# A mixture-of-experts kernel in which experts of 128 and of 64 slots alternate

## The reference, cut to what matters

```python
def _clamped_swiglu(hgu):
    x_glu = jnp.minimum(hgu[..., ::2], SWIGLU_LIMIT)
    x_lin = jnp.clip(hgu[..., 1::2], -SWIGLU_LIMIT, SWIGLU_LIMIT)
    return x_glu * jax.nn.sigmoid(SWIGLU_ALPHA * x_glu) * (x_lin + 1.0)

def _moe_sequence(h, ...):
    logits = h @ w_router + b_router
    top_val, top_idx = lax.top_k(logits, TOP_K)
    gates = jax.nn.softmax(top_val, axis=-1)
    ...                      # rows sorted by expert, group_sizes rows each
    hgu = lax.ragged_dot(xs, w_gate_up, group_sizes) + b_gate_up[e_sorted]   # 1024 -> 2048
    act = _clamped_swiglu(hgu)
    out = lax.ragged_dot(act, w_down, group_sizes) + b_down[e_sorted]        # 1024 -> 1024
    out = out * gates...
    return jax.ops.segment_sum(out, tok, num_segments=L)
# after it: h = _layernorm(2**0.25 * h + moe, ln2_g, ln2_b)
```

## Time and profile before

| | |
|---|---|
| three runs | 1982.99, 1983.78, 1988.11 us (median 1983.78) |
| profiled execution | 1988.11 us |
| its span, first to last instruction | 1986.4 us |
| TensorE clock granted, mean | 0.983 of full speed |
| PE, DVE, ACT, POOL busy | 97%, 86%, 69%, 24% of the span |
| DMA | 533.04 MB, mean 268 GB/s |

### The profile page before, as it was taken

One profiled execution on the slowest core, in us unless ns is written; L12 is line 12 of the kernel. 1 busy time (PEld: TensorE's weight loads), 2 busy tenths in 40 slices (PEclk: granted clock), 3 DMA queues, 4 the chain that ended last, 5 costly groups with the idle time before them and its releaser, 6 DMA issues.

```text
span 1986.4 us, 29687 instructions
## 1 busy us (share of the span) xinstructions
PE 1934.8 (97%) x8812; PEld 1543.5 (78%) x8812; DVE 1704.4 (86%) x1768; ACT 1372.6 (69%) x1742; POOL 468.4 (24%) x339
## 2 busy tenths in 40 slices
PE   6999999998989999999999999999999999999998
PEld 3657767787768887888888888888888888888886
DVE  6899977358855478999999999999999999999998
ACT  4456855224345526888888888888888888888885
POOL 6671000000000108323222232222322222222231
PEclk7999999999989988999999999999999999999999
DMA  8222225332010257999999999999999999999995
GB/s 318 79 107 84 85 100 181 124 100 81 22 43 23 64 170 267 376 388 376 374 380 369 388 372 375 385 371 387 373 378 382 362 387 370 376 384 363 384 373 213
DMA packets 152207, 533.04 MB, mean 268 GB/s; under 512 B 14479, under 2 KB 19759, under 8 KB 149408
## 3 DMA queue, kind: packets, MB, share of 16 engines
q1 hardware_dynamic: 136112, 492.45, 65.6%
q0 software_dynamic: 16048, 39.99, 7.8%
HBM read 517.75 MB, written 24.26 MB: 273 GB/s over the span
## 4 chain that ended last, share of the span: by engine, by line
PE 89%; DVE 7%; DMA 1%; issue 1%; ACT 1%; SPq 0%; DVEq 0%; ACTq 0%
PE ps L980 55%; PE ps L1127 4%; PE ps L1175 4%; PE ps L918 3%; PE ps L1118 3%; PE ps L1156 2%; PE ps L1132 2%; PE ps L1351 2%; PE ps L1223 2%; PE ps L886 2%; PE ps L1017 2%; PE ps L857 1%; DMA arena<-in_w_down 1%; PE ps L1105 1%; PE ps L871 1%
## 5 line engine op out<-in xcount | busy, mean ns | idle before, releaser
L980 PE MATMUL ps<-split,xTs 128*128 128x512 f32 x3264 | 771.1, 392 | 0.7 <-ACT split L1799 0.5
L980 PEld LDWEIGHTS ps<-split,xTs 128*128 128x128 f32 x3264 | 610.8, 188 | 131.2 <-DVE split L2551 1.5
L2551 DVE TENSOR_TENSOR split<-arena,split 128x2048 fp32r<-128x2048 f32 x204 | 464.0, 2287 | 49.7 <-ACT split L1799 49.6
L1799 ACT ACTIVATE split<-arena 128x1024 fp32r<-128x1024 f32 x408 | 409.8, 1054 | 106.0 <-PE ps L980 104.6
L2551 DVE TENSOR_TENSOR split<-ring,split 128x2048 fp32r<-128x2048 f32 x204 | 465.7, 2314 | 0.4 <-ACT split L1799 0.3
L1799 ACT ACTIVATE split<-ring 128x1024 fp32r<-128x1024 f32 x408 | 410.9, 1055 | 66.7 <-PE ps L980 53.7
L980 PE MATMUL ps<-split,aTs 128*128 128x512 f32 x1632 | 385.9, 392 | 0.2 <-DVE split L2551 0.2
L980 PEld LDWEIGHTS ps<-split,aTs 128*128 128x128 f32 x1632 | 303.7, 188 | 63.4 <-DVE split L2551 0.9
L728 POOL DMA_INDIRECT arena<-h_rows,slots x33 | 92.8, 2811 | 340.0 <-PE ps L918 244.8
L776 POOL DMA_INDIRECT y_rows<-arena,slots x33 | 94.0, 2848 | 176.3 <-issue 104.9
L1961 DVE TENSOR_TENSOR split<-ring,split 128x2048 fp32r<-128x2048 f32 (+1 forms) x32 | 72.7, 2273 | 63.4 <-ACT split L1462 63.4
(11 more groups left out here) (437 smaller groups left out, 2539.0 us busy)
## 6 DMA issues: line engine op xcount, KB each, us to landing
ring<-in_w_gate_up SPq DMA_DIRECT2D x170, 1024.0 KB, 8.8
arena<-in_w_gate_up SPq DMA_DIRECT2D x102, 1024.0 KB, 7.3
arena<-in_w_down SPq DMA_DIRECT2D x102, 1024.0 KB, 10.3
ring<-in_w_down SPq DMA_DIRECT2D x34, 1024.0 KB, 10.8
ring<-in_w_in SPq DMA_DIRECT2D x23, 1024.0 KB, 5.0
ring<-in_w_out SPq DMA_DIRECT2D x8, 1024.0 KB, 5.4
ring<-in_mod_w SPq DMA_DIRECT2D x10, 512.0 KB, 9.1
ring<-in_mod_w SPq DMA_DIRECT2D x4, 1024.0 KB, 5.0
```

Of the source, the lines that this page charges most:

```text
L980: m = mm(ps[:, banks + q, :], lhs[:, x_, k, :], w[:, q * 512:(q + 1) * 512], start=start, stop=stop)
L1799: A(split[:, 0, c % SPLITS, :], chunk(c), ACT.Copy).then_inc(sig("hi_ready"), 1)
L2551: V.tensor_tensor(split[:, 1, s_, :].rearrange("p a b -> p (a b)"), chunk_pair(p), split[:, 0, s_, :].rearrange("p a b -> p (a b)"), ALU.s ...
```

## The change

1. The sixteen experts with the most rows (and expert 0 always) are *big*, 128 slots; the others are *small*, 64 slots. They alternate: item 0 big, then big and small in turn, then the last small one and, one by one, what is over (64 slots each) in a loop of its own. The code for an item is so laid down several times, the loop over 14 pairs of a big and a small item in the middle.
2. A small item has its 64 high columns and 64 low columns side by side in one stationary operand. One matmul then gives x_hi*w_hi and x_lo*w_hi in the upper and lower 64 rows of PSUM, a pair is 8 matmuls and not 12. Before the activation the halves are added: ACT copies PSUM to `comb` (`rows_out`), and 8 matmuls against two identities side by side (`turn_sum`) add and turn it at once. The activation of a half is then 128x256, already turned. The down product's two halves are not added but scattered one after the other, the second when the first has landed.
3. In a small item two of the down pairs (8 and 9, `WHOLE`) are not split: PE multiplies the chunks as plain fp32, 4 matmuls each.
4. Unused slots point out of bounds and are left out by the scatter. A small item gathers 64 rows.
5. The four down tiles are loaded as `(p k)`: each partition takes two neighbouring rows, a piece of 8 KB. The activation is turned to match.
6. The list of items by size comes from DVE (`key`, `max`, a scan) and one matmul, and DVE reads the order straight from PSUM. What is over is listed by POOL (`late_list`), once, in the middle of its loop.
7. `y_dram` begins as plain `h1` (4 DMAs, earlier). The gates are divided by `ALPHA` and the epsilon by its square. `gates@b_down` is added at the end, in the PSUM banks of the last sum.

```diff
+WHOLE = (8, 9)
@@ expert_tile
-                sp.dma_start(x..., src.rearrange("o (k p) n -> p (o k) n", p=P)).then_inc(tile_ready[j % SLOTS], 16)
+                rows = "o (k p) n -> p (o k) n" if j < 8 else "o (p k) n -> p (o k) n"
+                sp.dma_start(x..., src.rearrange(rows, p=P)).then_inc(tile_ready[j % SLOTS], 16)
@@ POOL
+            for t in range(TC):
+                pool.dma_start(y_dram[t * P:(t + 1) * P, :], h1[:, t, :]).then_inc(sig("y_begun"), 16)
...
-            for c in range(TC):
-                pool.wait_ge(sig("acc"), 2 * (c + 1))
-                pool.dma_start(y_dram[c * P:(c + 1) * P, :], h1[:, c, :]).then_inc(sig("y_begun"), 16)
...
+            def item_rows(it, before_small):
+                m = it.i
                 wait_alone(pool, sig("xt_ps"), pool.to_reg(m * 2 + 2))
                 wait_alone(pool, sig("slot_g_in"), pool.to_reg(m * 16))
+                gather(idx_g[0:HALF_SLOTS, :] if it.next_small else idx_g)
+                wait_alone(pool, sig("y_ready"), pool.to_reg(m + 0))
+                if before_small:
+                    scatter(0, HALF_SLOTS)
+                    wait_alone(pool, sig("scattered"), pool.to_reg(it.rows - 16))
+                    scatter(HALF_SLOTS, P)
+                else:
+                    scatter(0, P)
                 wait_alone(pool, sig("gathered"), pool.to_reg(m * 16 + 32))
...             # slot_g; slot_s once scattered; hi_used; eo, as before
+            item_rows(big_item(0), False)
+            for lo, hi in ((0, LOOPS // 2), (LOOPS // 2, LOOPS)):
+                with pool.Fori(lo, hi) as k:
+                    item_rows(small_item(k), False)
+                    item_rows(big_item(k + 1), True)
+                if lo == 0:
+                    late_list()
+            item_rows(small_item(LOOPS, True), False)
...
+            with pool.Fori(1, n_late) as j:
+                item_rows(late_item(j), True)
@@ POOL, late_list: 42 operations of up to 128x256, nearly all one after the other, then
+                for w in range(2):
+                    pool.dma_start(list_dram[w:w + 1, :]..., late_i[0:LIST, w:w + 1]...).then_inc(sig("late_in"), 16)
+                pool.wait_ge(sig("late_in"), 32)
+                for w, dst in enumerate((eint, bint)):
+                    pool.dma_start(dst[0:1, E:E + LIST], list_dram[w:w + 1, :]).then_inc(sig("late_in"), 16)
+                pool.wait_ge(sig("late_in"), 64)
@@ PE
+                            m = product(c, banks, lhs, k + step * n_, 0, 0, start and n_ == 0, False)
+                            if not it.small:
+                                ...
+                                m = product(c, banks, lhs, k + step * n_, 1, 0, False, False)
...
+                    def whole_pair(p, banks, lhs, k, start, within=None):
+                        pe.wait_ge(tile_ready[p % SLOTS], ...)
+                        for n_ in range(2):
+                            w = chunk(2 * p + n_)
+                            for q in range(2):
+                                m = mm(ps[:, banks + q, :], lhs[:, 0, k + 2 * n_, :].bitcast(F32), w[:, q * 512:(q + 1) * 512], ...)
+                        m.then_inc(sig("whole_used"), 1)
...
+                    def turn_sum(half):
+                        pe.wait_ge(sig("comb"), it.at * 2 + (half + 1))
+                        for o in range(2):
+                            for k in range(4):
+                                m = mm(ps[:, 6, at:at + HALF_SLOTS], comb[:, o, ...], both_halves, start=True, stop=True)
+                        m.then_inc(sig("at_ps"), 1)
...
+                    # small: up(0..4), turn_sum(0), up(5..7), down(8) with turn_sum(1) within,
+                    #        down(9) with turn_next within, down(10), down(11)
+                    # big: as before
@@ ACT, small items: split_high leaves out chunks 16 to 19
+                rows_out(0)
+                split_high(12, 14)
+                sigmoid(0)
+                split_high(14, 16)
+                act_high(0)
+                split_high(20, 22)
+                rows_out(1)
+                split_high(22, 24)
+                sigmoid(1)
+                act_high(1)
+                next_high()
@@ DVE: begin_rows is gone; small items split pairs 0 to 7, 10 and 11
@@ end of PE: shares(t) opens each bank of the last sum
```

More of the change, by code:

```diff
@@ L322, in program @@
         logit = m3.take(TC, E)
[L323 to L329, removed]
+        order_row, odd_row, even_row = m3.take(E), m3.take(E), m3.take(E)
+        key, key_rest, count, large, ahead, seat, seat_d, second = (m3.take(E) for _ in range(8))
+        at_seat = m3.take(E)
+        best8, next8 = m3.take(8), m3.take(8)
+        evb = m3.take(P)
+        posm1 = m3.take(TC)
+        both_halves = m3.take(HALF_SLOTS)
         v8 = m3.take(TC, 8)
         if4 = m3.take(TC * TOPK)
-        place, over, over_x = m3.take(TC * TOPK), m3.take(TC * TOPK), m3.take(TC * TOPK)
-        blist = m3.take(ITEMS)
+        place, over = m3.take(TC * TOPK), m3.take(TC * TOPK)
+        late_i = m3.take(2)
         gates = m3.take(TC, TOPK)
@@ L1023, in experts, with bias @@
[L1023 to L1029 removed]
+                    def bias(half):
+                        if half == 0:
+                            pe.wait_ge(sig("eo_ready"), i + 1)
+                        for q in range(2):
+                            mm(ps[:, 2 * half + q, :], eo[:], bgu[:, half * D + q * 512:half * D + (q + 1) * 512], start=False, stop=False)
@@ L1031, in rows_so_far, with shares @@
+                def shares(t):
+                    for q in range(2):
+                        mm(ps[:, SUM_BANK[t] + q, :], gT[:, t * P:(t + 1) * P], bdown[:, q * 512:(q + 1) * 512], start=True, stop=False)
                 def rows_so_far(t, lo, hi):
@@ new lines, in next_low @@
+                def next_low():
+                    for q in range(2):
+                        dve.wait_ge(sig("xt_hi"), i * 2 + 3 + q)
+                        low(xTs, q, 7 - 6 * q, sig("xt_lo"), it.next_small)
+                for p in range(6):
+                    split_low(p)
+                if not it.small:
+                    activation(0)
+                    split_low(6)
+                    split_low(7)
+                    act_low(0)
+                    split_low(8)
+                    activation(1)
+                    split_low(9)
+                    act_low(1)
+                    split_low(10)
+                    split_low(11)
+                    next_low()
+                    return
```

646 lines of the change are left out of this document (409 added, 237 removed).

## The result

The changed kernel takes 2075.8 us against 1983.4: ratio 1.046 (1.041 to 1.051), slower by 92 us where 52 less had been forecast. It is the median of three runs; a fourth took 2158.1 us at a lower granted clock and is left out. The profiled execution has a span of 2066.8 us.

The account below looks back on a forecast made before the run. PE bound the old kernel, DMA the new: 33.9 us an item, not 35.48, over 34 items -53.7; `late_list` +3, start -2.5, tail +1: -52.2 from 1988.1, less 4.3 for a median: 1932 us, range 1893 to 1976.

Parts of the forecast that it names:

- The term for late tiles: Weight tiles between big and small items: six slots carry 1.8 us, late tiles add 0.2 us, giving 33.9 an item.
- TensorE in a small item, 25.2 us: PE's work in a small item: split pairs 18.2, whole pairs 3.4, bias 0.92, turns 2.6; sum 25.2 us.
- ACT 28.1 and DVE 27.6 us: Splits, activation and output in a small item: these two engines, not PE, bound it at some 28.5 us.
- DMA sets the pace at 33.7 us an item: Weights, scatter, gather and overhead need 33.7 us an item (33.0 to 34.6), more than the engines' 31.8.
- `late_list`, +3 (0 to 20): List made once in POOL's queue, some 35 us with 26 of cover; costs +3 us, 0 to 20.
- 8 KB pieces, 0.2 us an item: Four down tiles of an item load at 421, not 407 GB/s: 10.3 us become 10.0, or 10.3; 0.2 taken.
- valid rows 0.9: Scatter of valid rows only: the DMA's scatter share of an item falls from 2.6 to 1.7 us.
- Scatter chain, 0: POOL's wait for the first half's scatter before the second is covered by slack: zero, up to 3 us per pair.
- Start, -2.5: Before the items: `begin_rows` and ACT's empty output go, early `y_dram` writes; -2.5 us (+3 to -6).
- The clock (D, 2% of 9): Rival: PE's gaps at each tile lower the clock in small items, 25.2 becomes 50 us, +300; 2% of slower's 9%.

Follow-up runs that it names:

- 1: Changed kernel with only the order on ScalarE and VectorE altered, `rows_out(1)` ahead of the split: 2000.5 us, ratio 1.007 to the kernel before.
- Kernel 11: Kernel 5 with the second chunk of each plain down pair left out, 8 plain matmul instructions per small item, not 16: 1950.4 us, ratio 0.982.
- kernel 2: Changed kernel without the late list's operations and DMAs, the number of late items a constant: 2062.8 us, ratio 1.039 to the kernel before.
- kernel 5: Changed kernel with the order of 1 and the late list in seven parts, one behind every second pair of items: 1981.1 us, ratio 0.9991.
- 4: Changed kernel with the down tiles loaded in 4 KB pieces as before: 2084.8 us, ratio 1.049 to the kernel before.
- 12: Kernel 5 with the second scatter of a small item's rows and the wait for the first left out: 1974.3 us, ratio 0.994.
- kernel 17: Kernel with pairs 2 and 9 plain and list in parts (1976.4 us), the list now moved from SBUF to SBUF, not through DRAM: 1970.8 us, ratio 0.9933.

## Why the prediction was wrong

The failing step is this sentence: "Six slots of tiles can carry the 1.8 us by which a big item's PE is slower than the DMA into the small one. I add 0.2 for tiles that come late where that doesn't quite work." The term for late tiles was 0.2 us an item, 33.9 in all or 67.8 a pair; the pairs took 71.5 to 76.8. The sentence took a stock of tiles for granted and did not follow one tile from the moment its slot is free to its use. Two pairs that ScalarE skips bring the next tile's use forward by two pairs of splits, and the pairs that TensorE reads raw hold their slots longer. In ScalarE's order of instructions that late tile stood ahead of `rows_out(1)`, so TensorE waited 2.1 to 3.1 us in nearly every small item. Shown by 1: 75 us of the 92. The lower clock is a part of them: the pairs of the change that had it are some 2 us longer than the pairs that hadn't (means 74.9 and 72.9, the first pair left out), 16 us in eight of them, an estimate.

- *TensorE in a small item, 25.2 us.* It is 30.5: fp32 products of `mm` are two instructions each. The earlier trace rows gave the duration of an instruction and I multiplied it by matmuls of the source. The trace of before had the answer: `rows_so_far` has 8 matmuls in the source and 16 at its line. Kernel 11, with the 8 that I had counted, gains 31 us, part of it by slots that come free earlier.
- *ACT 28.1 and DVE 27.6 us.* Right within some 4%: over a pair of items DVE has 59.5 to 60.2 busy and ACT 55.4 to 55.5, where the working gives 33.3 + 27.6 and 29.6 + 28.1.
- *DMA sets the pace at 33.7 us an item.* Half right. In the mended kernels the share is 1.00, but over one pair only 377 to 382 GB/s were moved and 85 us less loading gives 18. A share of 1 was no proof, as the text itself had said, and the conclusion leaned on it all the same. TensorE's own 65.9 us (35.4 + 30.5) and the DMA's 67.4 (2 x 33.7, an estimate of the working) lie close together, and the pairs take 69.4 to 70.4; that the waits of the two add up is my reading.
- *`late_list`, +3 (0 to 20).* 13 by kernel 2 and 19 by kernel 5 (15 and 16 by the ratios), inside its range. The list took 53 us, not 35. Of some 45 short operations at least twelve took 2.1 to 2.7 us.
- *8 KB pieces, 0.2 us an item; valid rows 0.9.* The first is not decided by 4. The second was not separated.
- *Scatter chain, 0.* Near: one scatter less gives 7 us in all (12), not over 60; by what, the DMA or the wait, that run doesn't tell.
- *Start, -2.5.* The bias of the second item stands at 791.51, before at 798.05: -6.5.
- *The clock (D, 2% of 9).* Given as a whole item at half speed, which did not come. It fell for 3 to 7 us in eight of fourteen small items, behind one wait of 2 to 3. The Trainium skill, "TensorE: Matmul & The Clock Gate", section "HAM oscillation — how this bites in real kernels", describes waits for the next weights between short runs of matmuls, each followed by the low clock. The trace agrees in part: 0.50 at 1836 to 1840 behind such a wait, but 1.00 throughout behind the like waits of six items. A chance of 2% on it was too small with a wait that the order of ScalarE made sure of.

The account from 2075.8 down: order 75, late list in parts 19, plain pairs apart 5, list within SBUF 6, to 1970.8. From there to the forecast of 1932 are 39 us, and the miscounted plain matmuls are up to 31 of them (measured on the base of 5, not on kernel 17, and with slots freed earlier). The other 8 or more stay open.

## What to carry to other kernels

When a change takes steps out of one engine's list, follow the next transfer: from what frees its buffer, through its landing, to the instruction that needs it, and look at what is queued behind that instruction. Count instructions in the trace, not in the source, before multiplying by a duration. Where two resources are within 3% of each other, forecast their waits on top and not the larger of the two.

## What the runs showed of the hardware

- Two DMAs that store 32 words of 4 bytes each to DRAM held up the whole queue: 31 and 68 GB/s for 4 us in place of 410, and a weight tile landed after 18.45 us. In kernel 5's trace a gap stands at the same place of the list (53 GB/s at 1666 to 1667). The same words from SBUF to SBUF left none.
- Under load, GpSimd's operations on up to 32 columns took either 0.2 to 0.5 us or 2.1 to 2.7 (COPY of one column 2.13, of 16 columns 0.20). VectorE's split takes 2.29; that the one waits out the other is my reading, not shown.
- Tiles of 1 MB that were asked for in a bunch landed after 11 to 14 us, beside 8.2 before, with the same bytes or fewer.
- Waits of TensorE that were much alike, 2.1 to 3.1 us at the same place of a loop, were followed by a clock of 0.50 in eight small items and by 1.00 in six.
